# Splitting a chunk's weights in one instruction per engine in place of two

## The reference

```python
# first block
a = rms_norm(x, norm_mix)
q, k, v = split(a @ sb_w_qkv, 3)                 # 2048 x 6144
h = x + stick_breaking(q, k, v) @ sb_w_o
h = h + square(relu(rms_norm(h, norm_mlp) @ mlp_w1)) @ mlp_w2     # 8192 hidden
x = rms_norm(h, final_norm)
# second block
h = concat(meta_tokens, x)
u, gb, gc, v, ga, gbr = split(rms_norm_2(h, g) @ w_in)
y_a = grouped(causal_multiscale_pool(u), pool_w) * pool_scale
y_b = (gb * causal_depthwise_conv(gc * v, conv_w)) @ conv_out_w
h = h + (sigmoid(ga + ..) * y_a + sigmoid(gbr + ..) * y_b) @ w_o
gate, up = split(rms_norm_2(h, g) @ w_gate_up, 2)                 # 5632 hidden
out = rms_norm_2(h + (silu(gate) * up) @ w_down)[:, 16:]
```

## Time and profile before

| | us |
|---|---|
| median of 3 runs (2458.31 to 2458.97) | 2458.93 |
| the profiled execution | 2458.06 |
| its span, first to last instruction | 2456.3 |

### The profile page before, as it was taken

How to read it: one execution, slowest core, us unless ns; L and a number is a source line. 1 busy time by engine, 2 the same in 40 slices (tenths; PEclk the granted TensorE clock), 3 DMA queues, 4 the chain that set the end, 5 groups by cost and what they waited for, 6 DMA issues and landing times.

```text
span 2456.3 us, 40061 instructions
## 1 busy us (share of the span) xinstructions
PE 2445.1 (100%) x16053; PEld 2276.6 (93%) x16053; DVE 1647.5 (67%) x1413; ACT 1202.9 (49%) x1181; POOL 142.6 (6%) x87
## 2 busy tenths in 40 slices
PE   9999999999999999999999999999999999999998
PEld 9999999999999999999999999999999889988997
DVE  7577777656656666787765886666766556665665
ACT  6456555544444444544543345445554535443544
POOL 0000100000000000000200530000000000000001
PEclk9999999999999999999999999999999999999999
DMA  8655556666666666555655556666666566666664
GB/s 271 197 173 171 172 189 197 199 204 201 196 203 205 196 200 204 190 201 193 203 191 194 197 195 202 205 203 196 200 206 196 193 200 200 204 202 201 198 221 137
DMA packets 243962, 485.37 MB, mean 198 GB/s; under 512 B 7728, under 2 KB 8944, under 8 KB 243696
## 3 DMA queue, kind: packets, MB, share of 16 engines
q1 hardware_dynamic: 243520, 483.12, 60.1%
q10 hardware_dynamic: 320, 0.53, 0.1%
HBM read 481.53 MB, written 2.10 MB: 197 GB/s over the span
## 4 chain that ended last, share of the span: by engine, by line
PE 98%; DVE 1%; issue 0%; DMA 0%; ACT 0%; POOL 0%; SPq 0%; DVEq 0%; ACTq 0%; POOLq 0%
PE ps L1363 42%; PE ps L1370 21%; PE ps L1418 14%; PE ps L1397 8%; PE ps L1426 7%; PE ps L1403 4%; PE ps L1474 0%; PE ps L1440 0%; PE ps L1528 0%; DMA raw<-in_sb_w_qkv_dram 0%; PE ps L1462 0%; PE ps L1511 0%; PE ps L1533 0%; PE ps L1465 0%; POOL za L1246 0%
## 5 line engine op out<-in xcount | busy, mean ns | idle before, releaser
L809 DVE TENSOR_TENSOR wlo<-raw,whi 128x1024 fp32r<-128x1024 f32 x900 | 1144.9, 1284 | 757.4 <-ACT whi L601 756.3
L601 ACT ACTIVATE whi<-raw 128x1024 fp32r<-128x1024 f32 x900 | 947.9, 1056 | 1162.1 <-PE ps L1370 776.8
L1363 PE MATMUL ps<-b_buf,whi 128*128 128x512 f32 x2688 | 636.0, 379 | 0.0
L1363 PEld LDWEIGHTS ps<-b_buf,whi 128*128 128x128 f32 x2688 | 483.3, 190 | 54.1
L1370 PEld LDWEIGHTS ps<-b_buf,wlo 128*128 128x128 f32 x2688 | 352.3, 191 | 18.0
L1370 PE MATMUL ps<-b_buf,wlo 128*128 128x256 f32 x2688 | 354.2, 275 | 0.0
L1418 PE MATMUL ps<-a_buf,whi 128*128 128x258 f32 (+4 forms) x2560 | 313.3, 276 | 0.0
L1363 PE MATMUL ps<-c_buf,whi 128*128 128x512 f32 x1280 | 303.0, 380 | 0.0
L1418 PEld LDWEIGHTS ps<-a_buf,whi 128*128 128x128 f32 x2560 | 299.5, 191 | 0.3
L1363 PEld LDWEIGHTS ps<-c_buf,whi 128*128 128x128 f32 x1280 | 230.1, 190 | 25.7
L1363 PE MATMUL ps<-a_buf,whi 128*128 128x512 f32 x768 | 181.7, 379 | 0.0
(11 more groups left out here) (199 smaller groups left out, 1453.1 us busy)
## 6 DMA issues: line engine op xcount, KB each, us to landing
raw<-in_mlp_w_dram SPq DMA_DIRECT2D x128, 1024.0 KB, 5.2
raw<-in_w_in_dram SPq DMA_DIRECT2D x96, 1024.0 KB, 5.1
raw<-in_w_gate_up_dram SPq DMA_DIRECT2D x88, 1024.0 KB, 5.0
raw<-in_sb_w_qkv_dram SPq DMA_DIRECT2D x44, 1024.0 KB, 5.1
raw<-in_w_down_dram SPq DMA_DIRECT2D x44, 1024.0 KB, 5.1
raw<-in_sb_w_o_dram SPq DMA_DIRECT2D x16, 1024.0 KB, 5.1
raw<-in_conv_out_w_dram SPq DMA_DIRECT2D x16, 1024.0 KB, 5.1
raw<-in_w_o_dram SPq DMA_DIRECT2D x16, 1024.0 KB, 5.1
```

The costliest lines, as they stand in the source:

```text
L601: act.activation(whi[:, unit_of(n, u)], raw[:, n % RAW, u * UK:(u + 1) * UK, :], ACT.Copy).then_inc(w_hi, 1)
L809: dve.tensor_tensor(wlo[:, s], raw[:, n % RAW, u * UK:(u + 1) * UK, :], cast(whi[:, s]), ALU.subtract).then_inc(w_lo, 1)
L1363: pe.matmul(ps[:, 4 * half + j, :].rearrange("p (c n a) -> p c n a", c=2, a=2), whi[:, unit_of(n, u), kt, j * P:(j + 1) * P], parts_by_tur ...
```

## The change

`split_hi` and `split_lo` work on a chunk instead of on a unit. ScalarE waits once, for both units of the chunk two before to be used, and its one instruction of 2,048 columns raises `w_hi` by two. VectorE waits once, for both, and its one instruction of 2,048 columns raises `w_lo` by two. What TensorE waits for stays the same, and so do the buffers, SP's waits and the first panel.

```diff
+        def chunk_of(part, n):
+
+            s = unit_of(n, 0)
+            return part[:, s:s + UNITS].rearrange("p s t n -> p (s t n)")
...
                 act.wait_ge(raw_landed[n % RAW], landed_count(cnt, ahead))
-                for u in range(UNITS):
-                    if cnt.i is not None or n * UNITS + u >= SPLIT:
-
-                        act.wait_ge(w_used, cnt.at("chunk", ahead) * UNITS + (u + 1 - SPLIT))
-                    act.activation(whi[:, unit_of(n, u)], raw[:, n % RAW, u * UK:(u + 1) * UK, :],
-                                   ACT.Copy).then_inc(w_hi, 1)
+                if cnt.i is not None or (n + 1) * UNITS > SPLIT:
+                    act.wait_ge(w_used, cnt.at("chunk", ahead) * UNITS + (UNITS - SPLIT))
+                act.activation(chunk_of(whi, n), raw[:, n % RAW].rearrange("p t n -> p (t n)"),
+                               ACT.Copy).then_inc(w_hi, UNITS)
...
                 dve.wait_ge(raw_landed[n % RAW], landed_count(cnt, ahead))
-                for u in range(UNITS):
-                    dve.wait_ge(w_hi, cnt.at("chunk", ahead) * UNITS + (u + 1))
-                    s = unit_of(n, u)
-                    dve.tensor_tensor(wlo[:, s], raw[:, n % RAW, u * UK:(u + 1) * UK, :], cast(whi[:, s]),
-                                      ALU.subtract).then_inc(w_lo, 1)
+                dve.wait_ge(w_hi, cnt.at("chunk", ahead) * UNITS + UNITS)
+                dve.tensor_tensor(chunk_of(wlo, n), raw[:, n % RAW].rearrange("p t n -> p (t n)"),
+                                  cast(chunk_of(whi, n)), ALU.subtract).then_inc(w_lo, UNITS)
```

## The result

The kernel after took **2489.74 us** in the median of 4 runs (2488.66 to 2490.90), beside 2458.95 for the kernel before (4 runs). The ratio is 1.0127 with a 95% interval of 1.0115 to 1.0138: 30.8 us slower, where 19.3 were forecast and the range ended at 2488. The profiled execution took 2490.07, its span is 2488.3, 32.0 longer than that of before.

The account below looks back on a forecast made before the run. The prediction took TensorE to bound the kernel, so only its waits count. Eight terms of added waiting sum to 19.3 us: 2458.06 + 19.3 = 2477.4, about 2478 us as a median, range 2466 to 2488.

Parts of the forecast that it names:

- What bounds the kernel; the saved busy time is worth nothing: TensorE, busy 2445.1 of 2456.3 us; VectorE's and ScalarE's sums fall some 85 and 90 us without moving the end.
- The cost of one merged instruction: Each split of 2,048 columns: 1,917 ns on ScalarE, and an estimated 2.27 us on VectorE.
- Shift of 1.9 us at the end of a panel: Work in VectorE's queue behind a just-freed chunk's split comes 0.86 + 1.04 = 1.9 us later; bounds 0 and 2.3.
- Ordinary chunks lose nothing: In an ordinary chunk hi and lo are ready after 4.2 us, before TensorE wants them, so nothing is lost.
- the cover of 3.0: In an ordinary chunk, the 3.0 us between lo being ready and TensorE wanting it; hi has 1.2.
- The places of the sum: Losses at attention weights, softplus, first w_o panel's banks, norms, pool stage, last u panel, last down projection, tail: together 19.3 us.
- (f): Last u panel: six VectorE evacuations stand between two splits, and lo comes too late for TensorE, 2.0 us.
- (b): Softplus: L927 comes late behind the splits; 1.7 us in the first group, 0.4 in each other three, 2.9 together.
- Not slower: Rival: VectorE reaches chunks with both halves waiting, so merging shrinks existing waits, 1 us together; about 2458 us, chance 0.06.
- Only the waits that exist grow: Rival: only attention weights without the fourth group, second norm and pool stage lose, 9.5 us; 2468 us, chance 0.15.
- The exclusion on SBUF: Rival: in four convolution panels longer splits hold up POOL and lo comes late, 8 us in all; 2486, chance 0.13.
- The rule on breaking instructions up: Skill's sentence against the change: where unsaturated engines cause bubbles on others, smaller instructions may let work complete sooner; sign: slower.

Follow-up runs that it names:

- the repeat: The kernel after run once more, unchanged: 2490.19 us in one run, beside 2458.59 for the kernel before.
- the k panels reordered: Kernel after, with the merged split at the end of a k panel put behind evacuation and attention weights: 2480.22 us, ratio 1.0087.

## Why the prediction was right in its sign and too low

- *What bounds the kernel; the saved busy time is worth nothing.* Right: 93 and 80 us less (85 and 90 forecast), and the span grows.
- *The cost of one merged instruction.* Right: 1.92 us and 2.29 to 2.32, against 1.92 and 2.27.
- *Shift of 1.9 us at the end of a panel.* Too small by 0.2: 2.10. The handovers between the engines were left out, 0.19 at the k panel and 0.54 at the last u panel.
- *Ordinary chunks lose nothing.* Right but for one place: the differences stand still from 414.31 to the last w2 panels, and from 1277.82 to the last down projection but for the third norm. The same sentence said "even with three evacuation instructions of 1.23 us in between". That did not follow from its own numbers, as 3 x 1.23 = 3.7 is more than the cover of 3.0, and this is the place that the sum missed. Behind each of three of the last w2 panels VectorE has a low part and the squares of two norms between two splits, and TensorE lost 0.37 us for lo:

```profile
1018.93 1.22 DVE L1109 TENSOR_TENSOR a_buf<-full,a_buf 128x1024 f32 x1
1020.07 1.22 DVE L1114 TENSOR_TENSOR S<-S,S 128x1024 f32<-128x1024 f32 x1
1021.20 1.22 DVE L1114 TENSOR_TENSOR acc<-acc,U 128x1024 f32<-128x1024 f32 x1
1022.34 2.29 DVE L810 TENSOR_TENSOR wlo<-raw,whi 128x2048 fp32r<-128x2048 f32 x1
...
1024.68 1.16 PE L1371 MATMUL ps<-b_buf,wlo 128*128 128x256 f32 x8
```

- *The places of the sum.* All eight terms turned up, each 0.3 to 1.1 larger than forecast. (f) is the largest miss of one place, 2.9 for 2.0: the closing split in front of its chain ended 2.45 us later, not 1.9, and 0.26 had been lost ahead of it. In (b) the amount in the first group was nearly right, 1.5 for 1.7, and L927 came as late as forecast, 159.08 - 157.44 = 1.64 us:

```profile
159.08 1.76 DVE L928 TENSOR_TENSOR pp<-t,pp 128x1536 fp32r<-128x1536 f32 x1 [2.17 <-ACT pp L727]
```

But TensorE had lost 1.3 of these 1.5 us already, to hi and lo of a chunk behind the v panel (0.4 and 0.9), which the term did not have for this group.
- **The step that failed.** The prediction wrote "So 2458.06 + 19.3 = 2477.4": the sum of the waits was taken for the loss. It had no term for what TensorE does after a wait, and gave no reason for that. Of the 12.6 us between 31.9 and 19.3, 6.5 are products at 1.2 GHz, 4.9 are the eight terms mis-sized as above, 1.1 the place missed and 0.1 the start. With the waits alone, 25.3, the time would have been 2458.95 + 25.3 = 2484, inside the range. The profile of before showed the clock at 1.00, and that was taken for granted in a kernel whose waits were to grow to over 2 us. The Trainium skill (TensorE: Matmul & The Clock Gate, What's actually happening) has the clock at half or at full rate, depending on how busy the engine has been; the rows agree, 0.50 or 1.00.
- *The rivals.* Not slower: no, the split is preceded by 5.51 us of idle time. Only the waits that exist grow: no, new ones came at all the forecast places. The exclusion on SBUF gave 2486, close to the time, but that would have been luck: the first half of it happened and the second did not. One kind of POOL's instructions in the convolution panels got 1.08 us longer in the mean, about the 1.04 that the rival had (before, after):

```profile
L1226 POOL TENSOR_TENSOR S<-S,S 128x1024 f32<-128x1024 f32 x4 | 12.9, 3236 | 0.3
...
L1227 POOL TENSOR_TENSOR S<-S,S 128x1024 f32<-128x1024 f32 x4 | 17.2, 4312 | 0.3
```

POOL is busy 20.9 us more over the whole program (163.5 against 142.6), but no lo came late there: while POOL works on the four convolution panels, TensorE is busy throughout, before and after (columns as above):

```profile
1361.00:1442.00 81.00, 81.00 (x667) 79.26 (x667) 76.78 (x37) 31.81 (x31) 57.52 (x20) 1.00 0.57 193
...
1392.00:1475.00 83.00, 83.00 (x671) 80.86 (x671) 54.51 (x23) 30.28 (x17) 64.36 (x20) 1.00 0.60 200
```

- *The rule on breaking instructions up.* The Trainium skill (Perfetto Trace Analysis, Optimizing Scalar/DVE Operations) has the sign that was measured. But length is not all of it: 12.4 of the 30.8 us are lost with all instructions as short as before and the wait alone made coarser.

## What to carry to other kernels

On an engine that waits for buffers to come free, the grain of the release decides how late all that stands behind it in the queue is; merge instructions only where nothing urgent follows, or put the urgent chain ahead (9.5 us here with the same instructions). When a sum of waits takes TensorE's longest wait beyond those that the trace of before shows at full clock, add a price for slower products behind it, and give the range an end with it and one without.

## What was not expected of the hardware

The granted clock. Over the thirteen profiles of this case (the repeat left out), TensorE had 25 waits of 2.00 to 2.69 us; 13 were followed by a stretch at 1.2 GHz, 12 were not. No wait of 1.94 us or less was, away from the first and the last microseconds; all five of 3.47 us or more were, two of them for about 3.4 us and three for 6.8 (in these three the clock fell 0.5 to 1.6 us before the wait had ended). A stretch of 3.4 us cost some 1.5 to 1.8 us. Within that middle band the length alone does not decide: 2.12 us gave a stretch twice and none once in the same run, 2.52 gave one in the kernel after and none with the k panels reordered. What does decide there was not settled.
